# Two input projections on 512 tokens by seven block products, and modulation sums moved beside the output products

## What is computed

```python
sh1, sc1, g1, shm, scm, gm, sh2, sc2, g2 = split(silu(c) @ ada_w[layer] + ada_b[layer], 9)   # modulation
h = h + 0.5 * g1 * swiglu(prenorm(h, norm, sh1, sc1), ffn1_w_in[layer], ffn1_w_out[layer])   # hc in the same way
...                                                                                          # mixer
h = h + 0.5 * g2 * swiglu(prenorm(h, norm, sh2, sc2), ffn2_w_in[layer], ffn2_w_out[layer])   # hc where layer == 0

def swiglu(h, w_in, w_out):          # w_in 1024 x 5632, w_out 2816 x 1024
    g, u = split(h @ w_in, 2)
    return (silu(g) * u) @ w_out
def prenorm(h, gain, shift, scale):
    return rmsnorm(h, gain) * (1 + scale) + shift
```

## Time and profile before

| | us |
|---|---|
| median of three runs | 2954.96 (2953.32 to 2960.80) |
| span of the profiled execution | 2958.5 |
| PE busy | 2902.9 (98%) |
| DVE busy | 1932.3 (65%) |
| ACT busy | 1315.1 (44%) |
| DMA moved | 439.36 MB, mean 149 GB/s |

### The profile page before, as it was taken

One profiled execution on the slowest core, in us unless ns is written; L12 is line 12 of the kernel. 1 busy time (PEld: TensorE's weight loads), 2 busy tenths in 40 slices (PEclk: granted clock), 3 DMA queues, 4 the chain that ended last, 5 costly groups with the idle time before them and its releaser, 6 DMA issues.

```text
span 2958.5 us, 51029 instructions
## 1 busy us (share of the span) xinstructions
PE 2902.9 (98%) x19572; PEld 2562.6 (87%) x19572; DVE 1932.3 (65%) x3058; ACT 1315.1 (44%) x1952; POOL 0.2 (0%) x4
## 2 busy tenths in 40 slices
PE   9999999999999999999999999999999999999999
PEld 6888878887788878888888999999899999998998
DVE  5856763647748676334676667677776776787666
ACT  4332333423222332223335655555655555556555
POOL 0000000000000000000000000000000000000000
PEclk9999999999999999999999999999999999999999
DMA  8635642055546545332323665455456645554564
GB/s 248 199 116 175 192 128 86 30 157 157 161 138 185 167 143 150 102 94 85 114 86 99 190 182 162 139 164 172 143 148 194 187 133 159 160 169 138 164 192 135
DMA packets 614437, 439.36 MB, mean 149 GB/s; under 512 B 22172, under 2 KB 578040, under 8 KB 614136
## 3 DMA queue, kind: packets, MB, share of 16 engines
q1 hardware_dynamic: 613268, 436.70, 50.0%
q10 hardware_dynamic: 996, 0.23, 0.0%
HBM read 430.84 MB, written 1.05 MB: 146 GB/s over the span
## 4 chain that ended last, share of the span: by engine, by line
PE 87%; DVE 8%; ACT 1%; issue 1%; SPq 1%; DMA 1%; DVEq 0%; ACTq 0%
PE ps L476 27%; PE ps L478 26%; PE ps L477 26%; DVE wlo L425 2%; ACT whi L418 1%; PE ps L1834 1%; DVE normed L2726 1%; DMA raw<-ffn_w_in 1%; PE ps L1846 1%; SPq L745 1%; PE ps L891 1%; PE ps L1814 1%; DVE xl L2718 1%; PE ps L996 0%; PE ps L1300 0%
## 5 line engine op out<-in xcount | busy, mean ns | idle before, releaser
L476 PE MATMUL ps<-xh,whi 128*128 128x256 f32 (+1 forms) x3744 | 1206.6, 322 | 23.6 <-DVE xl L2718 4.5
L477 PE MATMUL ps<-xl,whi 128*128 128x256 f32 (+1 forms) x3744 | 1185.2, 317 | 0.0
L478 PE MATMUL ps<-xh,wlo 128*128 128x256 f32 (+1 forms) x3744 | 1184.9, 316 | 0.0
L425 DVE TENSOR_TENSOR wlo<-raw,whi 128x1024 fp32r<-128x1024 f32 x732 | 868.7, 1221 | 178.2 <-ACT whi L418 175.3
L418 ACT ACTIVATE whi<-raw 128x1024 fp32r<-128x1024 f32 x731 | 747.9, 1054 | 457.7 <-PE ps L478 378.6
L476 PEld LDWEIGHTS ps<-xh,whi 128*128 128x128 f32 x3744 | 706.3, 189 | 106.3 <-issue 43.2
L478 PEld LDWEIGHTS ps<-xh,wlo 128*128 128x128 f32 x3744 | 706.9, 189 | 50.9
L477 PEld LDWEIGHTS ps<-xl,whi 128*128 128x128 f32 x3744 | 707.0, 189 | 48.7
L476 PE MATMUL ps<-hid_h,whi 128*128 128x512 f32 (+1 forms) x1056 | 353.3, 335 | 0.2 <-DVE wlo L425 0.2
L478 PE MATMUL ps<-hid_h,wlo 128*128 128x512 f32 (+1 forms) x1056 | 352.0, 333 | 0.0
L477 PE MATMUL ps<-hid_l,whi 128*128 128x512 f32 (+1 forms) x1056 | 351.8, 333 | 0.0
(11 more groups left out here) (387 smaller groups left out, 2618.8 us busy)
## 6 DMA issues: line engine op xcount, KB each, us to landing
raw<-ffn_w_in SPq DMA_DIRECT2D x176, 512.0 KB, 5.4
mod_pair<-ada_w SPq DMA_DIRECT2D x48, 1024.0 KB, 5.3
raw<-w_in SPq DMA_DIRECT2D x96, 512.0 KB, 4.5
raw<-w_ffn_in SPq DMA_DIRECT2D x88, 512.0 KB, 4.7
raw<-w_gate SPq DMA_DIRECT2D x64, 512.0 KB, 3.9
mod_w<-ada_w SPq DMA_DIRECT2D x24, 1024.0 KB, 10.5
raw<-ffn_w_out SPq DMA_DIRECT2D x64, 384.0 KB, 4.0
raw<-ffn_w_out SPq DMA_DIRECT2D x64, 320.0 KB, 3.7
```

Of the source, the lines that this page charges most:

```text
L425: nc.vector.tensor_tensor(split_at(unit, wlo, s, h), raw[:, s, h, :], split_at(unit, whi, s, h).bitcast(F32), ALU.subtract).then_inc(S("lo ...
L476: nc.tensor.matmul(dst, w_h, x_h, start=start, stop=False)
L477: nc.tensor.matmul(dst, w_h, x_l, start=False, stop=False)
L478: return nc.tensor.matmul(dst, w_l, x_h, start=False, stop=stop)
```

## The change

The input products of the second and third FFN are made by Strassen's scheme in Winograd's form, after the first two pairs of hidden tiles. One **quad** stands for two hidden tiles: gate and up by latent and context tokens, with the 1024 features in two halves, is a product of 2x2 blocks, made in seven steps of 24 matmuls of 256 columns instead of 96 of 512. 4 quads are in the first half, 5 in the second. The sums of weights are made partly by loads that add (issued by GpSimd onto landed weights, `sum_quads`), partly by DVE (`add`); the sums of inputs once for each FFN by DVE (`t_sums`), split in high and low by ACT and DVE. The seven products are put together by DVE out of PSUM (`plus`). Weights go through seven slots (`quad_roles`), of which three are new.

Since DVE has this to do there, the modulation sums leave those input products. `MOD_DOWN` puts 14 of the 24 pairs beside output products of the three FFNs, `MOD_BESIDE` keeps ten in the first FFN. `down_pair` holds two quarters of a pair, `down_acc` one accumulator. Some semaphores are shared under new names (`small_ready`, `small_by_act`, `sum_for_act`), with the same waits.

```diff
-MOD_BESIDE = {("ffn1", 0): ((0, 8, 5), (0, 18, 5)), ("ffn2", 0): ((1, 4, 5), (1, 14, 5)), ("ffn1", 1): ((1, 28, 4), None)}
-MOD_AT_NORM = {"mix": (0, 28, 4, 3, 4), "ffn2": (0, 32, 8, 5, 6), "ffn1": (1, 24, 4, 3, 4)}
+MOD_BESIDE = {("ffn1", 0): ((0, 8, 5), (0, 24, 5))}
+MOD_DOWN = {("ffn1", 0): ((0, 18, 3), (0, 34, 1)), ("ffn2", 0): ((1, 12, 3), (1, 18, 2)), ("ffn1", 1): ((1, 26, 3), (1, 32, 2))}
+MOD_AT_NORM = {"mix": (1, 0, 4, 3, 4), "ffn2": (1, 4, 8, 5, 6), "ffn1": (1, 22, 4, 3, 4)}
+NORM_DOWN = {"mix": 2, "ffn1": 4}
...
+QUAD, STEPS = 4, 7
+QUAD_BANKS = (4, 5, 1, 3)
...
+        down_acc = [Region(at)(f"down_acc{j}", [P, 2, 4 * P]) for j, at in enumerate((sq2_at, overlay + tail))]
+        down_pair = Region(first.at)("down_pair", [P, 2, 2, 4 * P])
...
+        def quad_roles(quads):
+            roles = [dict(a11=0, s3=1, a22=2, a12=3, s1=4, f1=5, f2=6)]
+            for _ in range(quads - 1):
+                o = roles[-1]
+                roles.append(dict(s1=o["f1"], s3=o["f2"], a11=o["s1"], a22=o["s3"], a12=o["a11"], f1=o["a12"], f2=o["a22"]))
+            return roles
+        STEP_ROLE = ("a11", "a11", "s1", "a12", "s3", "a12", "a22")
...
+            def load_quads(v, j0, quads, after_down, rows_before):
+                u0 = c.units
+                free = {0: half_free(0, u0, 0), 1: half_free(0, u0, 1), 2: half_free(0, u0 + 1, 0), 3: half_free(0, u0 + 1, 1),
+                        4: half_free(0, u0, 0), 5: step_seq(u0, 0) + HALF_CREDIT, 6: step_seq(u0, 0) + HALF_CREDIT}
...
+                for q, role in enumerate(quad_roles(quads)):
+                    if q == 1 and after_down:
+                        sp.wait_ge(S("mm_done"), 2 * u0 + HALF_CREDIT)
+                    for name, source in (("a11", "a11"), ("s3", "a21"), ("a22", "a22"), ("s1", "a21"), ("a12", "a12")):
+                        again = step_seq(u0, STEPS * (q - 1) + used[name]) + HALF_CREDIT if q else 0
+                        sp.wait_ge(S("lo_ready"), max(free[role[name]], again))
+                        if q == 0 and name == "s1":
+                            sp.wait_ge(S("mod_rows_mm"), rows_before)
+                        for s in range(2):
+                            sp.dma_start(quad_place(role[name], s), quad_weights(v, j0 + 2 * q, s, source))\
+                                .then_inc(S(LANDED[name]), 16)
...
+            def mod_down(layer, m0, pairs):
+                before = c.of["mod_pairs"]
+                c.add(mod_pairs=pairs)
+                def load(i, s):
+                    for part in range(2):
+                        quarter = 2 * s + part
+                        if is_first(i, s):
+                            sp.wait_ge(S("hid_l_ready"), c.hidden + CREDIT)
+                        else:
+                            sp.wait_ge(S("mod_step"), mod_summed(before + i - (not s), 4 * ((quarter + 2) % 4) + 4))
+                        sp.dma_start(down_pair[:, part], mod_pair_columns(layer, i * 2 + m0, s)[:, 2 * part:2 * part + 2])\
+                            .then_inc(S(f"mod_landed{part}"), 16)
+                return load
...
+                    load = mod_down(*down_mods[n]) if down_mods[n] else None
+                    if load:
                         for p in range(4):
...
+                            for s in range(2):
+                                for h in range(2):
+                                    after_quads = free[2 * s + h] if shift is not None and p == 0 else 0
+                                    sp.wait_ge(S("lo_ready"), max(half_free(0, c.units + s, h), after_quads))
+                                    sp.dma_start(raw[:, s, h, 0:half * P // 2].rearrange("p (k n) -> p k n", n=P),
+                                                 columns(w_out, j0, half, 2 * p * P, P, P)(0, s, h))\
+                                        .then_inc(S(f"raw_landed{s}{h}"), 16)
+                            for s in range(2):
+                                if p < down_mods[n][2]:
+                                    load(p, s)
+                            c.units += 2
+                            if n == 1 and at_norm and shift is not None and p == 0:
+                                sp.wait_ge(S("mm_done"), 2 * (c.units - 2) + HALF_CREDIT)
+                            if n == 1 and at_norm:
...
+            def sum_quads(v, j0, quads, u0):
+                for q, role in enumerate(quad_roles(quads)):
+                    for name, source in (("s3", "a11"), ("s1", "a22")):
+                        if name == "s1":
+                            pool.wait_ge(S("s1_base"), 32 * (c.of["quads"] + q + 1))
+                        else:
+                            pool.wait_ge(S(LANDED[name]), 16 * ((u0 + QUAD * q) // 2 + 2))
+                        for s in range(2):
+                            pool.dma_start(quad_place(role[name], s), quad_weights(v, j0 + 2 * q, s, source),
+                                           accum_op=ALU.add).then_inc(S(f"{name}_landed"), 16)
...
+            def mod_down(part, n):
+                layer, m0, pairs = part
+                group, before = mod_group(layer, m0), c.of["mod_pairs"]
+                c.add(mod_pairs=pairs)
+                def rows(pair):
+                    if pair == 0:
+                        pe.wait_ge(S("mod_copied"), group)
+                    pe.wait_ge(S("mod_step"), mod_summed(before + pair, MOD_STEPS))
+                    for u in range(2):
+                        for j in range(2):
+                            to, g = 2 * (2 * pair + u) + j, 32 * (2 * u + j)
+                            m = nc.tensor.matmul(ps[g:g + 32, 6, 0:2 * P], mod_sel[:, 31 - to:63 - to],
+                                                 down_acc[n][:, j, u * 2 * P:(u + 1) * 2 * P],
+                                                 start=pair == 0, stop=pair == pairs - 1)
+                    m.then_inc(S("mod_rows_mm"), 2)
+                def before_unit(i, s):
+                    if s == 0 and 1 <= i <= pairs:
+                        rows(i - 1)
+                    elif s == 1 and i == pairs:
+                        pe.wait_ge(S("mod_copied"), group + 1)
+                        pe.wait_ge(S("mod_evac"), MOD_UNITS * layer + m0)
+                        mod_turned(mod_row, 7).then_inc(S("mod_mm"), 1)
...
+                for r in range(STEPS * count):
+                    q, m = divmod(r, STEPS)
...
+                    pe.wait_ge(S("lo_ready"), step_seq(u0, r) + HALF_CREDIT)
...
+                    for s in range(2):
+                        for k in range(DC // 2):
+                            ins = three(ps[:, QUAD_BANKS[r % 4], s * T:(s + 1) * T], w_h[:, s, k, :], w_l[:, s, k, :],
+                                        x_h[:, k, :], x_l[:, k, :], s == 0 and k == 0, s == 1 and k == DC // 2 - 1)
+                    ins.then_inc(S("mm_done"), 1 + (m == STEPS - 1))
...
+            def mod_down_sums(n, layer, m0):
+                before, landed = c.of["mod_pairs"], c.of["mod_landed"]
+                def sums(i, s):
+                    pair = before + i
+                    for part in range(2):
+                        dve.wait_ge(S(f"mod_landed{part}"), 16 * (landed + 2 * i + s + 1))
+                        if s == 0 and part == 0:
+                            dve.wait_ge(S("mod_rows_mm"), MOD_UNITS * layer + m0 + 2 * i)
+                        for x in range(2):
+                            k = 4 * s + 2 * part + x
+                            for j in range(2):
+                                acc, weight = down_acc[n][:, j, :], cond[:, k, 30 + j:31 + j]
+                                if k == 0:
+                                    ins = nc.vector.tensor_scalar(acc, down_pair[:, part, x, :], weight, None, ALU.mult)
+                                else:
+                                    dve.wait_ge(S("mod_step"), mod_summed(pair, 2 * k + j - 1))
+                                    ins = nc.vector.scalar_tensor_tensor(out=acc, in0=down_pair[:, part, x, :],
+                                                                         scalar=weight, in1=acc, op0=ALU.mult, op1=ALU.add)
+                                ins.then_inc(S("mod_step"), 1)
+                return sums
...
+            def t_sums(b):
...
+                for j in range(4):
+                    if j in (1, 3):
+                        dve.wait_ge(S("norm_prod"), c.of["norm_prod"] + j)
+                    for k in range(DC // 2):
+                        low, top = normed[:, k, :], normed[:, k + DC // 2, :]
...
+                        ins = nc.vector.scalar_tensor_tensor(out=t_sum[j][:, k, :], in0=in0, scalar=scalar, in1=in1, op0=ALU.add, op1=op1)
+                    ins.then_inc(S("norm_prod"), 1)
...
+                def first_steps():
+                    low(0)
+                    add(0, 1)
+                    low(1)
+                    low(2)
+                def run():
+                    for r in range(steps + 2):
+                        q, m = divmod(r, STEPS)
```

(63 more changed lines are left out.)

385 lines of the change are left out of this document (321 added, 64 removed).

## The result

| | us |
|---|---|
| kernel before, median | 2957.88 (2953.32 to 2963.56) |
| changed kernel, median | 3138.94 (3137.23 to 3142.57) |
| ratio | 1.0605, 95% interval 1.0593 to 1.0617 |
| span of the profiled execution, before / after | 2958.5 / 3135.4 |

The prediction was 3042 us, 2945 to 3085. The direction was right, the loss came out twice as large, and the time lies outside the range.

A forecast was written before the change was run, and what follows sets the result against it. PE, busy 2902.9 of 2958.5 us, was taken to bound the kernel. 2958.5 - 48.8 + 12.4 + 115 + 8.5 = 3045.6, less 3.5 from span to median, gave 3042 us, range 2945 to 3085.

The forecast's parts named there:

- Bound and place: PE sets the end; it waits for DVE after norms and before row products, with nothing put for DVE within quads.
- Quads, -48.8: Seven-step input products: 18.95 us of PE work per two hidden tiles instead of 21.66, 18 times, -48.8 us.
- Loads that add, 0: GpSimd's adding loads in the seven-step stages hide under PE's work: 0 us.
- the loop of s1: Seven-step weight slot: loads, adding, ACT and DVE work until free again, 12.7 us + X, hidden under 18.95 us.
- X: Seven-step stages: time from base load landed to both adding loads landed, taken as 5 to 6 us.
- my signs: Trace signs of right or wrong, among them seven steps over 20 us with DVE never idle as wrong.
- The rival: Seven-step stages: adding loads bind, landing in 10.5 us, 60 us more, 3102 us; chance 0.2.
- Sums of the input, +12.4: After two norms: t_sums on DVE stand behind a split, so PE waits 6.2 us twice, +12.4 us.
- Sums beside output products, +115: Output products: PE waits before row products for DVE's modulation sums and late weight loads, 14 pairs, +115 us.
- prefetch holds: Output products: next weights arrive in time, only DVE's work counts, some 35 us, 2954 us; chance 0.1.
- Clock, +8.5: Lower PE clock after waits, showing after the last pair of five stages, 1.7 us each, +8.5 us.

The follow-up runs named there:

- the second edit: Changed kernel with s3's base load first in SP's queue, waiting for the previous quad's adding load instead of its step 4 split: 3101.7 us.
- the third edit: Changed kernel with t_sums moved on DVE ahead of the split that waits for ACT, in both norms: 3121.9 us.
- The first run: Changed kernel with the output weights of pair p+1 issued on SP ahead of the second modulation load of pair p: 3050.8 us.
- e9: Changed kernel with all input products plain as before, modulation sums still beside the output products: 3101.0 us.
- e10: Changed kernel with matmuls that nothing reads put in front of the row products to fill PE's waits: 3138.5 us.
- e4: Changed kernel with output weights issued earlier, s3's base load issued earlier and t_sums ahead of the split, all together: 3002.3 us (ratio 1.0148).

## Why the prediction was wrong

- **Bound and place.** Right for the output products and the input sums: PE sets the end and waits for DVE where I put it, or runs slower behind such waits. Wrong within the quads: 31.6 us of waits where I had put nothing, and 9.5 at their ends.
- **Quads, -48.8.** Mis-sized. At 0.1178 a quad takes 19.79 us, and 96 matmuls of 512 columns, 0.2267 us from start to start, take 21.76, so 18 quads win (21.76 - 19.79) x 18 = 35 us. (My 0.1128 and 0.2256 divide a stretch by its count, which takes in the matmuls across its ends; from start to start they are 0.1133 and 0.2267.) I took the pace from the quickest stretch of before, while PEld at 60.00 of 60 us there said that nothing was spare in that pace. Besides, the ends were missing: at each of four stages PE waits 1.6 to 4.2 us (9.5 in all) for the last tiles, put together out of seven products. With both and all else removed as far as the runs did it, the input stages win some 17 us without the row products.
- **Loads that add, 0.** This is the step that failed, worth 37 us. I wrote the loop of s1 as 12.7 + X and let it hide under a whole quad. The one that bound is s3's: the second edit lets only s3's base load go earlier, and the quads fall to PE's pace. The time at hand is not a quad but the three steps between the split that lets the base load go and the sum that needs it, 8.1 us, and in it stand base (4.6) and X. X itself I took as 5 to 6, near plain loads of this size; it was 8.3, of which adding is 2.3. The bounds (4.2 to 10.5) held it, the choice between them did not. Of my signs this one showed in part: quads of 23.8 us and DVE idle for 5.4 us before the sum. An estimate by the Trainium skill (DMA: Bandwidth & Descriptors, Anatomy of one DMA) was 5.2 us for two in line, against 8.3 here; nothing in it is about adding. The rival was named with 60 us for X = 10.5, and this case lies nearest to the measured time.
- **Sums of the input, +12.4.** Right to 0.1 us as a wait; 4 us of lower clock behind it were missing, and the third edit gave 17.
- **Sums beside output products, +115.** Right: 102.7 in the trace, and pair by pair within 3 us but for one, the first of the first FFN (11.9 for 8.3). The eight later pairs of a stage all wait less than forecast, 4.2 us on average for 6.2. The first run shows the reason given, SP's order, and with it 37.7 us where the rival *prefetch holds* had 35.
- **Clock, +8.5.** Too small. I put 1.7 us at five places; the table of the change has six stages with sums, and behind a long wait it is 2.1. Waits and lower clock in the output products make 102.7 + 37.2 = 140 us where 115 + 8.5 = 123.5 stand, and in e9 they make the whole 141. How the missing 16 us divide between my two terms is not shown. That the later pairs wait 2.0 us less than forecast, about what the pair before has lost to the clock, fits what I said, that inside a stage DVE's chain covers it; e10 was too weak to test that.
- **The sum.** 87 forecast; + 13 for the pace, + 37 for the adding loads, + 4 and + 16 at the input sums and the output products, and, estimated from the waits of 9.5 us and the lower clock behind some of them, 10 to 15 at the ends of the quads make 167 to 172 of the 177 between the spans.
- **The range** ended at 3085 because it took in half of the case with slow adding loads. That case had 0.2, and with the clock at its upper bound it would have reached 3118. The failed step alone, put right, would have made 3079; that the time lies outside the range takes the pace, the ends and the clock too, each too small in the same direction.

## What to carry to other kernels

When a load waits for an event of the round before, measure the time from that event to the first use, not the length of the round; one wait that is stricter than the data need cost 37 us here, and one queue order 88. Work moved beside another stage brings its loads with it, and these stand in an in-order queue in front of that stage's own. Before an algebraic saving is counted, price its weight sums, its assembly and its ends: here 49 us on paper were at most 35 in matmuls and 7 in time, with everything else nearly free.

## What the runs showed of the hardware

- A load that adds onto data in SBUF lands after 6.7 us where the same load without adding takes 4.4 (256 KB, medians), after 5.7 where the base load was issued earlier (e2); two in line, behind a base load, 8.3 us after it.
- Matmuls of 256 columns with a new weight tile each ran mostly at 0.1133, 0.1178 or 0.1200 us at full granted clock, in long steady stretches. One difference came with an offset of 64 bytes of the weights (0.1178 and 0.1200), the other has no cause shown.
- Around each of the 24 waits of PE of 2.4 us and more in the changed kernel the granted clock fell to 1.2 GHz, within the wait or at most 1.1 us behind it. With shorter ones it did so at times: behind 1.99 us there, but not behind one of 2.34 us in e4 or of 2.08 us in e10.
